# Weight remainders, tanh gates, the adaptive rows' landing place and the opening's small loads in a three-layer kernel

## The chip, the cores and the metric

One NeuronCore of one Trainium2 chip runs the whole program. The metric is the device time of one execution in microseconds; the kernel before took 2408.9 us (median of 3 runs, 2406.74 to 2418.69).

## The reference, cut to what matters

The program runs one layer of a first kind and two of a second on 256 tokens of width 1024. All sums below are of the first layer; the second kind isn't touched, except for where its small vectors are loaded.

```
mod = silu(c) @ w_ada + b_ada            # 6 x 1024 values, from one row c (and c_ctx)
h   = rmsnorm(x) * (1 + scale) + shift   # 256 tokens, and 256 context tokens
q, k, v (attention), q, k, v, o, gates (mLSTM), g_na, g_ml = h @ w_in
a   = neighbourhood attention(q, k, v, context)      # 8 heads
m   = mLSTM(q, k, v, gates), both directions, head norm, * sigmoid(o)   # 4 heads
y   = (sigmoid(g_na) * (a @ w_branch_na) + sigmoid(g_ml) * (m @ w_branch_ml)) @ w_out
x  += gate * rmsnorm(y)
x  += gate * rmsnorm(experts(x))         # 32 experts of 3 x 1024 x 1024, 4 a token
```

## The kernel before, in words

**Engines.** Each engine has its own instruction stream, in program order; semaphores join them. SyncE (SP) issues the weight loads, ScalarE (ACT) issues the small loads at the start and then computes, GpSimd (POOL) issues a few loads, VectorE is DVE, TensorE is PE.

**The ring.** Weights pass through `ring`, 6 slots of 2 MB. `slabs` lists them in order, and slab n goes to slot n % 6; `freed(n)` gives the group of matmuls after which its slot may be overwritten. Four slabs `ada0` to `ada3` hold the first 2048 columns of `w_ada`. Behind the list come the expert slabs, six for each expert (`expert_slab`), j = 0, 1 for `w_gate`, 2, 3 for `w_lin` and 4, 5 for `w_down`.

**Rounded weights and remainders.** A product in float32 is made of three in the faster rounded format: ScalarE writes the rounded weights (`rounded1`, line 740), VectorE the remainder, weight less rounded weight (`rest1`, line 2027), and TensorE multiplies rounded by rounded, rounded by remainder and remainder by rounded. A 1 MB slab has its rounded copy in its own slot; a 2 MB slab (`nav`, `mlv`) has it in the next one (`nav_hi`).

**The rows of w_ada.** `ada0` to `ada3` are multiplied on TensorE (`ada`), copied to SBUF by ScalarE (`ada_copy`, line 716) and turned to columns by TensorE (`ada_turn`, line 1179). Rows 4 to 9 are loaded by GpSimd to `adaX`, two places of 1 MB (line 2701): both halves of a row are issued when the row before has been summed. VectorE sums them (`ada_part`, eight steps, lines 2056 and 2058) and TensorE folds the partitions (`ada_fold`, line 1217); `modulation` adds the bias. Rows 10 and 11 pass through the ring between the gate slabs, and their sums and folds stand in the attention heads (steps i = 1 to 15). The row they are summed in is `cossin`.

**Opening.** SyncE issues the tokens, `ada0`, and after the small vectors `ada1` to `ada3`, `nak0`, `nak1` and `nav`. ScalarE issues 2 + 8 + 1 small loads, and then 16 of the second kind's vectors (`VECS2`) and 10 constants. VectorE waits for the sigmoid of `c` (`sig_c`) ahead of the copies of the turned tokens (lines 1985, 1986). Then come the token norm, the four ada rows, the gains and the rounded tokens (lines 750, 751), and the attention keys, `na_k`, on TensorE (line 1253).

**Projections.** `tokens` (line 1268), `features` (1282) and `lat_pair` (1316) make the other products, with seven groups of small matmuls for the relative bias between them (`rel_group`, line 1230, copied by `rel_copy`) and the folds.

**Heads.** Step i is half qt = i % 2 of head h = i // 2. TensorE: scores of step i + 1 (1370), half of a gate projection (1316), on even steps `head_out` (1379), transposes of the probabilities (1398). VectorE: bias, maximum, scaling, and on odd steps the remainder of a gate slab. ScalarE: exp (803); on odd steps the sigmoid that empties gate h (759) and the rounding of gate h + 2; and the copy of the transposes (820).

**After the heads.** The mLSTM runs head by head with the branch product of attention between (1414, 1426, 1448, 1465); then come its branch product, the output projection (1541) with its norm sums (1501), the router and the experts (from about 440 us; their matmuls are lines 1598 and following). The experts' biases are rounded by ScalarE (892), and their remainder is made by GpSimd (2720). The angles for the second kind stand on VectorE between the remainder of `out3` and the first use of the output projection, which ScalarE's `c_pos` waits for.

## Time and profile before

| | |
|---|---|
| median, lowest, highest of 3 runs | 2408.9, 2406.74, 2418.69 us |
| the profiled execution | 2409.32 us |
| its span, first to last instruction | 2407.5 us |
| mean granted TensorE clock | 0.971 of full |
| TensorE busy | 2201.5 us, 91% |
| VectorE, ScalarE, GpSimd busy | 929.6, 734.7, 28.1 us |
| DMA | 626.98 MB, mean 260 GB/s |
| the first layer up to the experts | 0 to about 440 us |

Times in the rows are microseconds from the start of the span. In the time lines a row with a count merges equal instructions that follow each other, and the brackets give the engine's idle time before it and what ended it. In the busy times the numbers stand in the order PE, PEld (TensorE's weight loads), DVE, ACT, POOL, then the granted clock as a share of full speed, the mean busy share of 16 DMA engines, and GB/s.

### The profile page before, as it was taken

The numbers are of one execution on the slowest core, as the hardware profiler recorded it, in microseconds if no ns is written. First come the engines' busy times: TensorE is split into PE (matmuls) and PEld (weight loads), VectorE is DVE, ScalarE is ACT, GpSimd is POOL, SyncE is SP. The second block draws the span as 40 slices with busy tenths as digits, with TensorE's granted clock in tenths as the row PEclk, the third lists the DMA queues.
The fourth block names the chain that finished last, engine by engine and source line by source line (L and its number), as shares of the span: only waits on it lengthen the run. The fifth ranks groups of instructions, "written<-read, shape, count | busy, mean of one in ns | idle before, by whom it ended". The sixth has DMA issues, their size and how long they took to land.

```text
span 2407.5 us, 33072 instructions
## 1 busy us (share of the span) xinstructions
PE 2201.5 (91%) x13860; PEld 1569.3 (65%) x13860; DVE 929.6 (39%) x1355; ACT 734.7 (31%) x969; POOL 28.1 (1%) x32
## 2 busy tenths in 40 slices
PE   5999888999889888988998899999999799999998
PEld 4887676433333333333333488998999698998997
DVE  4456575311111121111121265366344454474453
ACT  4124552211101111111111245444433444544432
POOL 0000011000000000000000000000000000000000
PEclk8999998999999999999999999999999899999998
DMA  9462156699999999999999934544444454443542
GB/s 359 165 225 90 53 158 212 255 428 427 427 427 428 428 427 428 427 428 428 426 428 428 358 113 159 160 163 153 145 162 167 141 168 148 147 170 137 178 154 92
DMA packets 139388, 626.98 MB, mean 260 GB/s; under 512 B 7703, under 2 KB 33831, under 8 KB 114407
## 3 DMA queue, kind: packets, MB, share of 16 engines
q1 hardware_dynamic: 131808, 609.87, 65.0%
q0 software_dynamic: 5184, 13.90, 2.0%
q8 instruction: 120, 1.97, 0.3%
q10 hardware_dynamic: 2247, 1.01, 0.2%
q14 instruction: 29, 0.24, 0.0%
HBM read 623.69 MB, written 1.05 MB: 259 GB/s over the span
## 4 chain that ended last, share of the span: by engine, by line
PE 65%; DMA 23%; DVE 5%; issue 3%; ACT 3%; SPq 1%; ACTq 0%; DVEq 0%; POOL 0%
DMA ring<-in_w_lin 20%; PE bank L1598 15%; PE bank L1687 12%; PE bank L1922 10%; PE bank L1937 5%; PE bank L1845 3%; DMA ring<-in_w_in 2%; PE bank L1268 2%; PE bank L1316 2%; PE bank L1864 1%; DVE ring_rounded L2027 1%; PE bank L1711 1%; PE bank L1253 1%; PE bank L1696 1%; PE bank L1465 1%
## 5 line engine op out<-in xcount | busy, mean ns | idle before, releaser
L1598 PE MATMUL bank<-ring,arenaA 128*64 128x512 f32 x3072 | 692.9, 601 | 39.3 <-DMA ring<-in_w_lin 28.6
L1598 PEld LDWEIGHTS bank<-ring,arenaA 128*64 128x64 f32 x3072 | 211.0, 138 | 462.1 <-issue 390.3
L2475 DVE TENSOR_TENSOR ring_rounded<-ring,ring_rounded 128x2048 fp32r<-128x2048 f32 (+1 forms) x160 | 338.1, 2152 | 148.1 <-ACT ring_rounded L964 148.1
L964 ACT ACTIVATE ring_rounded<-ring 128x2048 fp32r<-128x2048 f32 (+1 forms) x160 | 280.4, 1799 | 284.7 <-DMA ring<-in_w_in 116.2
L1687 PE MATMUL bank<-arena_rounded,ring_rounded 128*128 128x256 f32 x2496 | 308.9, 284 | 0.0
L1687 PEld LDWEIGHTS bank<-arena_rounded,ring_rounded 128*128 128x128 f32 x2496 | 301.1, 190 | 4.1 <-issue 3.1
L1922 PE MATMUL bank<-arena_rounded,ring_rounded 128*128 128x256 f32 x2112 | 256.0, 282 | 1.2 <-DVE arena_rounded L2665 1.0
L1922 PEld LDWEIGHTS bank<-arena_rounded,ring_rounded 128*128 128x128 f32 x2112 | 252.8, 190 | 4.6 <-ACT arena_rounded L1106 3.0
L2421 DVE TENSOR_SCALAR arenaA<-bank 128x512 f32<-128x512 f32 x32 | 22.1, 692 | 502.4 <-PE bank L1598 502.4
L945 ACT ACTIVATE arenaA<-bank 128x512 f32<-128x512 f32 x32 | 19.1, 597 | 328.8 <-PE bank L1643 328.8
L1937 PE MATMUL bank<-arena_rounded,ring_rounded 128*128 128x256 f32 x912 | 110.0, 283 | 2.3 <-DVE arenaA L2677 2.3
L1937 PEld LDWEIGHTS bank<-arena_rounded,ring_rounded 128*128 128x128 f32 x912 | 109.5, 192 | 2.7 <-issue 2.7
L979 ACT ACTIVATE arenaA<-bank 128x512 f32<-128x512 f32 (+1 forms) x88 | 51.2, 586 | 188.8 <-PE bank L1687 86.9
L949 ACT ACTIVATE arenaA<-bank 64x512 f32<-64x512 f32 x64 | 37.9, 592 | 213.6 <-PE bank L1598 213.2
L943 ACT ACTIVATE arenaA<-arenaA 128x512 f32<-128x512 f32 x32 | 20.2, 630 | 266.3 <-DVE arenaA L2421 266.3
L2433 DVE TENSOR_SCALAR arenaA<-bank 128x512 f32<-128x512 f32 x32 | 22.1, 692 | 201.9 <-PE bank L1598 201.9
L1316 PEld LDWEIGHTS bank<-arena_rounded,ring_rounded 128*128 128x128 f32 x624 | 77.1, 193 | 12.5 <-issue 7.6
L2027 DVE TENSOR_TENSOR ring_rounded<-ring,ring_rounded 128x2048 fp32r<-128x2048 f32 x28 | 70.0, 2513 | 35.6 <-ACT ring_rounded L740 35.5
L1316 PE MATMUL bank<-arena_rounded,ring_rounded 128*128 128x256 f32 x624 | 81.0, 288 | 0.0
L2677 DVE TENSOR_TENSOR arenaA<-bank,arenaA 128x512 f32<-128x512 f32 x22 | 15.2, 691 | 145.5 <-PE bank L1922 145.3
L1611 PE MATMUL bank<-arenaA 128*128 128x256 f32 x256 | 63.5, 392 | 7.8 <-ACT arenaA L949 5.5
L1845 PE MATMUL bank<-arena_rounded,ring_rounded 128*128 128x256 f32 x576 | 70.5, 284 | 0.0
(385 smaller groups left out, 2210.6 us busy)
## 6 DMA issues: line engine op xcount, KB each, us to landing
ring<-in_w_gate SPq DMA_DIRECT2D x64, 2048.0 KB, 23.3
ring<-in_w_lin SPq DMA_DIRECT2D x64, 2048.0 KB, 25.6
ring<-in_w_down SPq DMA_DIRECT2D x64, 2048.0 KB, 21.8
ring<-in_w_in SPq DMA_DIRECT2D x34, 2048.0 KB, 12.0
ring<-in_w_ffn_gate SPq DMA_DIRECT2D x10, 2048.0 KB, 8.1
ring<-in_w_ffn_up SPq DMA_DIRECT2D x10, 2048.0 KB, 7.8
ring<-in_w_ffn_down SPq DMA_DIRECT2D x12, 1536.0 KB, 6.4
ring<-in_w_in SPq DMA_DIRECT2D x16, 1024.0 KB, 8.0
```

Source lines behind the costliest of these rows:

```text
L964: act.activation(place2(name + "_hi", ringR)[:, a:b, :], place2(name)[:, a:b, :], ACT.Copy).then_inc(w_hi, 1)
L979: act.activation(dst, src(b) if src else b, func, scale=scale).then_inc(c_act, 1)
L1268: last = pe.matmul(b[:, :], h(c), w[:, c, :], start=(part == 0 and c == 0), stop=(part == 2 and c == DC - 1), skip_group_check=True)
L1316: last = pe.matmul(b[:, j * T:(j + 1) * T], w[:, c, cols], h(c), start=(part == 0 and c == 0 and j == 0), stop=(part == 2 and c == kc - 1) ...
L1598: last = pe.matmul(bank[b][k * SLOTS:(k + 1) * SLOTS, :], lhsT(c), slot(j)[:, c % 4, k * 512:(k + 1) * 512], start=False, stop=(c == DC - ...
L1611: last = pe.matmul(bank[6 + g % 2][:, k * T:(k + 1) * T], yN[:, c // 4, (c % 4) * P:(c % 4 + 1) * P], selWT, start=True, stop=True)
L1687: last = pe.matmul(b[:, j * T:(j + 1) * T], w[:, c, m * P:(m + 1) * P], h[:, c, :], start=(part == 0 and c == 0 and j == 0), stop=(part == ...
L1845: last = pe.matmul(b[:, j * T:(j + 1) * T], wHL[w][:, c, m * P:(m + 1) * P], y[:, c, :], start=(part == 0 and c == 0 and j == 0), stop=(pa ...
L1922: last = pe.matmul(b[:, j * T:(j + 1) * T], w[:, c, m * P:(m + 1) * P], h[:, c, :], start=(part == 0 and c == 0 and j == 0), stop=(part == ...
L1937: last = pe.matmul(bank[m // 2][:, (m % 2) * T:(m % 2 + 1) * T], w[:, k, m * P:(m + 1) * P], h[:, c0 + k, :], start=(part == 0 and c0 + k ...
L2027: dve.tensor_tensor(lo[:, c, :], w[:, c, :], hi[:, c, :], ALU.subtract).then_inc(w_lo, 1)
L2475: dve.tensor_tensor(place2(name, ringR)[:, a:b, :], w[:, a:b, :], hi[:, a:b, :], ALU.subtract).then_inc(w_lo, 1)
```

## The change

- Opening: `VECS2` and the constants are issued by GpSimd; `mlgRaw` (64 bytes a row) goes behind the first row of `w_ada` there. The token copies of the first four chunks stand ahead of the silu. `VECS2` is turned later, in another bank, and eight matmuls of the identity follow the last `ada_turn`.
- `nak` is one slab of 2 MB with its rounded copy in slot 5.
- Rows 4 to 11 of `w_ada` all pass through `adaX`. Each half has its own semaphore and is loaded as soon as the half before it in that place has been summed. Eight folds stand in the projections, none in the heads; the list ends with two empty slots, and expert 0's slabs are issued in the order 4, 5, 0, 1, 2, 3.
- Heads: a gate is tanh(g / 2), and the products take it plus one; the factor 0.5 moves into `gpost` and the norm's scale. Slabs are rounded on even steps, one step ahead of their remainders; `bna0` and `bna1` are done inside the heads, and the slabs after them move one place ahead.
- The bias remainder is made by VectorE after the remainder of `out3`; ScalarE rounds the biases later.

The diff, cut to changed lines; the places are named:

```diff
# declarations
-adaRow = [Pna[:, 1, :] if i < 4 else wide(AT_MLO, 2, 512, arenaA)[:, i % 2, :] if i < 10 else cossin[:, :]
-          for i in range(12)]
+adaRow = [Pna[:, 1, :] if i < 4 else wide(AT_MLO, 2, 512, arenaA)[:, i % 2, :] for i in range(12)]
...
-ada_in = sem("ada_in")
+ada_in = [sem(f"ada_in{k}") for k in range(2)]
...
-slabs += [(f"nak{i}", half(C_NAK + 256 * i)) for i in range(2)]
-slabs += [("nav", w_in[:, :, C_NAV:C_MLK]), ("nav_hi", None),
+slabs += [("nak", w_in[:, :, C_NAK:C_NAV]), ("nak_hi", None), ("nav", w_in[:, :, C_NAV:C_MLK]), ("nav_hi", None),
...
-for k in range(8):
-    slabs += [(f"gate{k}", half(gate_at[k]))]
-    if k in (0, 2):
-        slabs += [(f"ada{10 + k // 2}", ada_src(10 + k // 2))]
+slabs += [(f"gate{k}", half(gate_at[k])) for k in range(8)]
...
+slabs += [(None, None)] * (-len(slabs) % RING)
...
+PIECES1 = {n: 2 if n in ("nak", "nav", "mlv") else 1 for n in SPLIT1}
# order of the PSUM groups
+ORDER1 = [f"na_k{m}" for m in range(4)] + ["na_v0", "na_v1", "ada4", "na_v2", "ada5", "na_v3", "ml_k0", "ada6", "ml_k1", "ada7",
+                                          "ml_v0", "ml_v1", "ml_v2", "ada8", "ml_v3", "ada9", "ml_g", "ml_q0", "ml_gt", "ada10",
+                                          "na_q0", "ada11", "na_q1", "ml_o0", "ml_o1"]
...
+groups += [("dve" if n.startswith("ada") or n == "ml_gt" else "act", n) for n in ORDER1 + GATES]
# freed, sync: expert 0's slabs
+    while slabs[n][0] is None:
+        n -= RING
...
-    for j in range(RING):
+    for j in (4, 5, 0, 1, 2, 3):
# scalar
-    for L in range(2):
-        for name, (r, k) in VECS2.items():
-            src = A[name][L]
-            src = src if len(src.shape) == 1 else src.rearrange("a b -> (a b)")
-            act.dma_start(vin2[L * NV2 + r:L * NV2 + r + k, :], src.rearrange("(a b) -> a b", b=P)).then_inc(vec2_in, 16)
-    for n in K:
-        if n not in FIRST:
-            act.dma_start(K[n][:, :], A[n]).then_inc(consts_in, 16)
...
-    act.wait_ge(vecs_turned, 2)
-    act.activation(v2T[:, :], bank[6][:, 0:2 * NV2], ACT.Copy).then_inc(v2_copied, 1)
...
+    act.wait_ge(vecs_turned, 2)
+    act.activation(v2T[:, :], bank[4][:, 0:2 * NV2], ACT.Copy).then_inc(v2_copied, 1)
...
-        if PIECES1[name] == 2:
+        if PIECES1[name] == 2 and S1[name + "_hi"] >= RING:
...
-    rounded1("nak0")
+    rounded1("nak", (0,))
...
-    rounded1("nak1")
+    rounded1("nak", (1,))
...
-            empty(GATES[h], dst, ACT.Sigmoid, src=two)
-            if h + 2 < 8:
-                rounded1(f"gate{h + 2}")
-            elif h == 7:
-                rounded1("bna0")
+            empty(GATES[h], dst, ACT.Tanh, scale=0.5, src=two)
+        elif h + 2 < 8:
+            rounded1(f"gate{h + 2}")
+        elif h == 6:
+            rounded1("bna0")
+        else:
+            rounded1("bna1")
...
-        if dr == 1:
-            rounded1(("bna1", "bml0", "bml1", "out0")[h])
+        if dr == 1 and h < 3:
+            rounded1(("bml0", "bml1", "out0")[h])
...
+    rounded1("out1")
...
-    rounded1("out1")
-    act.wait_ge(bias_in, 16 * 6)
-    act.activation(bparts, braw, ACT.Copy).then_inc(bias_hi, 1)
...
+    act.wait_ge(bias_in, 16 * 6)
+    act.activation(bparts, braw, ACT.Copy).then_inc(bias_hi, 1)
...
-        empty_post(bank[g % 4], m, sq2, mixT, gpost, 1.0, lin_act)
+        empty_post(bank[g % 4], m, sq2, mixT, gpost, 0.5, lin_act)
# tensor
-    pe.wait_ge(vec2_in, 16 * 2 * len(VECS2))
-    pe.transpose(bank[6][:, 0:2 * NV2], vin2[0:2 * NV2, :], K["ident"][0:2 * NV2, 0:2 * NV2]).then_inc(vecs_turned, 1)
...
-    pe.wait_ge(v2_copied, 1)
...
+    pe.wait_ge(vec2_in, 16 * 2 * len(VECS2))
+    pe.transpose(bank[4][:, 0:2 * NV2], vin2[0:2 * NV2, :], K["ident"][0:2 * NV2, 0:2 * NV2]).then_inc(vecs_turned, 1)
...
+    pe.wait_ge(v2_copied, 1)
+    for _ in range(8):
+        pe.matmul(bank[4][:, 0:P], K["ident"][:, :], K["ident"][:, :], start=True, stop=True)
...
-        pe.wait_ge(ada_sum, i - 3)
+        pe.wait_ge(ada_sum, 2 * (i - 3))
...
+            if part == 0 and k == 0:
+                wH, wL = highs("nak")
+            if part == 1 and k == 0:
+                lows("nak")
...
-    for t in range(3):
+    for t in range(2):
...
+    tokens("na_v", "nav", 2)
+    ada_fold(5)
...
-    ada_fold(5)
+    ada_fold(6)
...
-    tokens("ml_v", "mlv", 0)
-    tokens("ml_v", "mlv", 1)
-    ada_fold(6)
-    tokens("ml_v", "mlv", 2)
+    ada_fold(7)
+    for t in range(3):
+        tokens("ml_v", "mlv", t)
+    ada_fold(8)
+    ada_fold(9)
-    ada_fold(7)
...
-    ada_fold(8)
+    ada_fold(10)
...
+    ada_fold(11)
...
-    ada_fold(9)
...
-        if i in (8, 14):
-            ada_fold(9 + i // 7)
# vector
-    dve.wait_ge(sig_c, 1)
...
-    dve.tensor_tensor(scol[:, :, 0], vT[:, 0:8], stage[:, 0:8], ALU.mult)
-    dve.tensor_tensor(scol[:, :, 1], vT[:, 8:16], stage[:, 8:16], ALU.mult).then_inc(silu_done, 1)
...
+        if c == 4:
+            dve.wait_ge(sig_c, 1)
+            dve.tensor_tensor(scol[:, :, 0], vT[:, 0:8], stage[:, 0:8], ALU.mult)
+            dve.tensor_tensor(scol[:, :, 1], vT[:, 8:16], stage[:, 8:16], ALU.mult).then_inc(silu_done, 1)
...
-    rest1("nak0")
-    rest1("nak1")
+    rest1("nak")
...
-        if i < 10:
-            dve.wait_ge(ada_in, 32 * (i - 3))
-            w = lambda c: adaX[c // 4][:, c % 4, :]
-        else:
-            dve.wait_ge(*in1(f"ada{i}"))
...
+        w = lambda c: adaX[c // 4][:, c % 4, :]
...
+            if c % 4 == 0:
+                dve.wait_ge(ada_in[c // 4], 16 * (i - 3))
...
-            if c < DC - 1:
+            if c % 4 < 3:
...
+                if c == 3:
+                    dve.wait_ge(ada_sum, 2 * (i - 4) + 1)
...
-    ada_part(5, range(4))
+    ada_part(5, range(4, 8))
+    rest1("mlk")
-    ada_part(5, range(4, 8))
+    modulation(4)
+    ada_part(6, range(8))
-    rest1("mlk")
-    modulation(4)
+    modulation(5)
+    ada_part(7, range(4))
-    rest1("mlv", (0,))
+    ada_part(7, range(4, 8))
-    rest1("mlv", (1,))
-    modulation(5)
-    ada_part(6, range(4))
+    rest1("mlv")
+    modulation(6)
-    ada_part(6, range(4, 8))
+    ada_part(8, range(8))
+    modulation(7)
-    ada_part(7, range(8))
+    ada_part(9, range(8))
-    modulation(6)
...
...
-    ada_part(9, range(4, 8))
...
-        if i in (9, 15):
-            modulation(10 + i // 15)
-        if 1 <= i <= 4:
-            ada_part(10, range(2 * i - 2, 2 * i))
-        if 9 <= i <= 12:
-            ada_part(11, range(2 * i - 18, 2 * i - 16))
-        if qt and h + 2 < 8:
-            rest1(f"gate{h + 2}")
+        if qt:
...
-    rest1("bna0")
...
-        dve.tensor_tensor(merged[:, 2 * h:2 * h + 2, :], two(bank1(f"b_na{h}")[:, :]), gNA[:, 2 * h:2 * h + 2, :], ALU.mult)\
-            .then_inc(lin_dve, 1)
+        dve.scalar_tensor_tensor(out=merged[:, 2 * h:2 * h + 2, :], in0=gNA[:, 2 * h:2 * h + 2, :], scalar=1.0,
+                                 in1=two(bank1(f"b_na{h}")[:, :]), op0=ALU.add, op1=ALU.mult).then_inc(lin_dve, 1)
...
-        rest1(("bna1", "bml0", "bml1", "out0")[h])
+        if h < 3:
+            rest1(("bml0", "bml1", "out0")[h])
...
-        link(dve.tensor_tensor(gm, bank[g % 4][:, :].rearrange("p (a b) -> p a b", a=2), gm, ALU.mult))
+        link(dve.scalar_tensor_tensor(out=gm, in0=gm, scalar=1.0, in1=two(bank[g % 4][:, :]), op0=ALU.add, op1=ALU.mult))
...
+    dve.wait_ge(bias_hi, 1)
+    for k in range(2):
+        r = slice(64 * k + 32, 64 * k + 64)
+        dve.tensor_tensor(bparts[r, :, :], braw[r, :, :], bparts[r, :, :].bitcast(F32), ALU.subtract).then_inc(bias_lo, 1)
...
-    dve.tensor_tensor(gpost[:, :], mod[:, 16:24], vcol("g_mix_post"), ALU.mult)
+    dve.scalar_tensor_tensor(out=gpost[:, :], in0=mod[:, 16:24], scalar=0.5, in1=vcol("g_mix_post"), op0=ALU.mult, op1=ALU.mult)
# gpsimd
-    pool.dma_start(mlgRaw, w_in[:, :, C_MLG:C_NAQ]).then_inc(bg_in, 16)
-    for i in range(4, 10):
-        pool.wait_ge(*((lin_done, G1["ada3"] + 1) if i == 4 else (ada_sum, i - 4)))
+    for L in range(2):
+        for name, (r, k) in VECS2.items():
+            src = A[name][L]
+            src = src if len(src.shape) == 1 else src.rearrange("a b -> (a b)")
+            pool.dma_start(vin2[L * NV2 + r:L * NV2 + r + k, :], src.rearrange("(a b) -> a b", b=P)).then_inc(vec2_in, 16)
+    for n in K:
+        if n not in FIRST:
+            pool.dma_start(K[n][:, :], A[n]).then_inc(consts_in, 16)
+    pool.wait_ge(lin_done, G1["ada3"] + 1)
+    for i in range(4, 12):
-            pool.dma_start(adaX[k], ada_src(i)[:, 4 * k:4 * k + 4, :]).then_inc(ada_in, 16)
+            if i > 4:
+                pool.wait_ge(ada_sum, 2 * (i - 5) + k + 1)
+            pool.dma_start(adaX[k], ada_src(i)[:, 4 * k:4 * k + 4, :]).then_inc(ada_in[k], 16)
+        if i == 4:
+            pool.dma_start(mlgRaw, w_in[:, :, C_MLG:C_NAQ]).then_inc(bg_in, 16)
...
-    pool.wait_ge(bias_hi, 1)
-    for k in range(2):
-        r = slice(64 * k + 32, 64 * k + 64)
-        pool.tensor_tensor(bparts[r, :, :], braw[r, :, :], bparts[r, :, :].bitcast(F32), ALU.subtract).then_inc(bias_lo, 1)
```


## Rows read from the trace of the kernel before

**Rows 1.** The page, part 4: chain that ended last, by engine.

```profile
PE 65%; DMA 23%; DVE 5%; issue 3%; ACT 3%; SPq 1%; ACTq 0%; DVEq 0%; POOL 0%
```

**Rows 2.** By stage: stretch, length, busy us (instructions), granted clock, DMA share, GB/s.

```profile
72.86:201.30 128.44, 126.35 (x733) 107.29 (x731) 60.52 (x79) 34.10 (x35) 7.43 (x10) 0.93 0.62 212
201.30:306.00 104.70, 93.26 (x553) 69.68 (x552) 57.67 (x117) 55.43 (x79) 0.00 (x0) 0.92 0.18 57
```

**Rows 3.** Chain in order of time, opening: start us, us, what.

```profile
23.67 19.27 DMA ring<-in_w_in
42.96 1.37 ACT ring_rounded L740
...
49.09 23.77 PE bank L1253 x96
```

**Rows 4.** Time line, opening: start, us, engine, line, op, tiles, count [idle before].

```profile
1.95 0.90 POOL L2697 DMA_DIRECT2D arenaA<-in_w_in  x1
...
33.82 0.21 ACT L730 ACTIVATE colA<-colA 128x4 f32<-128x4 f32 x1
...
36.17 1.16 PE L1205 MATMUL bank<-k_ident,colA 128*128 128x128 f32 x8 [0.51 <-DVE colA L2007]
...
44.78 0.58 ACT L716 ACTIVATE arenaA<-bank 128x512 f32<-128x512 f32 x1
...
45.41 1.87 PE L1179 MATMUL bank<-k_pick,arenaA 128*128 128x2 f32 x8 [1.13 <-ACT arenaA L716]
```

**Rows 5.** Busy time in a stretch of the opening.

```profile
48.00:50.00 2.00, 0.91 (x2) 0.84 (x3) 2.00 (x2) 2.00 (x5) 1.08 (x2) 0.50 0.99 418
```

**Rows 6.** Time line, projections, TensorE and VectorE.

```profile
67.06 5.48 DVE L2058 SCALAR_TENSOR_TENSOR arenaA<-arenaA,scol 128x512 f32<-128x512 f32 x7
...
67.72 5.15 PE L1253 MATMUL bank<-arena_rounded,ring_rounded 128*128 128x512 f32 x22
...
88.84 7.39 PE L1268 MATMUL bank<-ring_rounded,arena_rounded 128*128 128x512 f32 x24
...
180.93 1.21 PE L1217 MATMUL bank<-ones,arenaA 128*128 128x1 f32 x8 [2.09 <-DVE arenaA L2058]
```

**Rows 7.** One line, GpSimd's ada halves: ns min/median/max, and us to landing.

```profile
L2701 POOL DMA_DIRECT2D arenaA<-in_w_ada x12: 748/751/770, 47.6 to 165.7; - x12
...
DMA to landing us min/median/max: 5.4/7.7/15.1
```

**Rows 8.** Time line, heads, ScalarE.

```profile
260.35 1.91 ACT L740 ACTIVATE ring_rounded<-ring 128x2048 fp32r<-128x2048 f32 x1 [9.99 <-DMA ring<-in_w_in]
```

**Rows 9.** Waits of TensorE, heads: us in total, times, longest.

```profile
PE bank L1379 <- ACT arenaA L820: 10.3, 2, 7.8
```

**Rows 10.** Time line, ScalarE: gates, softmax and table loads.

```profile
171.62 0.26 ACT L782 ACTIVATE arenaA<-arenaA 128x64 f32<-128x64 f32 x1
...
177.89 0.23 ACT L785 ACTIVATE arenaA<-arenaA 128x32 f32<-128x32 f32 x1 [4.07 <-DVE arenaA L2111]
...
214.07 1.28 ACT L759 ACT_TABLE_LOAD   x1 [2.89 <-PE bank L1316]
```

**Rows 11.** Time line, end of the heads.

```profile
300.20 1.94 PE L1379 MATMUL bank<-arenaA 128*64 128x256 f32 x8
...
308.54 3.33 PE L1379 MATMUL bank<-arenaA 128*64 128x256 f32 x8 [2.54 <-ACT arenaA L820]
...
312.37 2.29 DVE L2027 TENSOR_TENSOR ring_rounded<-ring,ring_rounded 128x2048 fp32r<-128x2048 f32 x1
...
320.44 1.16 PE L1426 MATMUL bank<-k_ident,arenaA 128*128 128x128 f32 x8 [0.79 <-ACT arenaA L852]
```

**Rows 12.** Time line, bias remainder and output projection.

```profile
375.32 9.03 POOL L2720 TENSOR_TENSOR arena_rounded<-arenaA,arena_rounded 32x1536 fp32r<-32x1536 f32 x2
375.62 10.87 DVE L2027 TENSOR_TENSOR ring_rounded<-ring,ring_rounded 128x2048 fp32r<-128x2048 f32 x2 [1.12 <-ACT ring_rounded L740]
...
391.72 1.07 PE L1501 MATMUL bank<-arenaA,ones 128*32 128x256 f32 x4 [7.68 <-ACT arenaA L879]
```

39 lines of the change are left out of this document (14 added, 25 removed).

## The prediction, written before the result was known

> **What bounds the kernel now.** I read the page first (the chain that ended last), then busy times by stage, then the chain in order of time and the time lines of the stages that the diff touches. The chain is mostly TensorE (PE), with DMA second [rows 1]; most of that DMA share lies in the expert layer, which no part of the diff makes shorter or longer: expert 0's slabs arrive long before their use, and the later ones are paced by the ring. So the question is by how much the work before about 440 us ends earlier or later; all behind it moves with it. Four stages matter. The opening (0 to 72.86 us) hangs on the transfer of `nak0` and `nak1`: one DMA piece of 19.27 us ends at 42.96 [rows 3]. The projections (72.86 to 201.3) are TensorE almost without a gap, 126.35 of 128.44 us. The attention heads (201.3 to 306) have 104.70 - 93.26 = 11.44 us without TensorE work [rows 2]. After them come short stretches in which TensorE waits for ScalarE or VectorE.
>
> **The change part by part.**
>
> *Opening, small loads.* ScalarE no longer issues 26 small DMAs, so its first ACTIVATE comes earlier; the token copies no longer stand behind the sigmoid. Neither moves the end of the opening: everything waits for `nak`, whose bytes stand in the same queue order. What helps `nak` is that 1024 rows of 64 bytes (`mlgRaw`, issued at 1.95 [rows 4]) no longer run ahead of it, and that it comes in rows of 2 KB instead of 1 KB. Neither has a row of its own. Below: no gain (the stream is as full as before), above: 3.5 us, a sixth of the 19.27 us piece [rows 3]. I take 1.1 us, near the lower end, because the bytes stay the same: landing at 41.9.
>
> *Opening, `nak` as one slab.* Before, `nak0` was rounded while `nak1` was on its way; after it landed only one rounding (1.82) stood before the copy of `ada3` at 44.78 [rows 3, 4]. Now nothing can be rounded until all has landed, and two roundings and the copy of `ada2` stand there: 1.82 + 0.60 + 1.82 = 4.24 instead of 1.82, so 2.4 us later. With the landing, the copy starts at 41.9 + 4.24 = 46.1, 1.3 us later than 44.78. Its followers keep their distances: the turn ended at 45.41 + 1.87 = 47.28 and `na_k` began at 49.09 [rows 3, 4].
>
> *Eight idle matmuls.* They stand on TensorE between the turn of `ada3` (now ending at 48.6) and `na_k`. Four like them take 1.16 us at the full clock [rows 4], so eight take 2.3 us, and 4.6 us at the half clock, which was granted here (0.50 from 48 to 50, [rows 5]). The cover is the 1.8 us between turn and tokens. I take them to end at 51.8, half of them slow, 1.4 us after the tokens are ready (50.4). They give back the slow start of `na_k`: 96 matmuls took 23.77 us [rows 3] and at the later pace (22 in 5.15 us [rows 6], some 0.237 each with the gaps) would take 22.75, 1.0 us less. Opening: +1.3 + 1.4 - 1.0 = +1.7 us; bounds -1.5 and +4.5.
>
> *Halved landing place, eight rows by GpSimd.* Two more `ada_fold` now stand in the projections, 8 matmuls each, 0.9 us: +1.8 us; they leave the heads, where the same 1.8 us goes. VectorE gets two more sums, 6.3 us each (a first step of 0.48 and seven, 5.48 us [rows 6]), into 68 us of idle time (128.44 - 60.52 busy [rows 2]). Each half waits for its own 1 MB, which takes 5.4 to 15.1 us to land, 7.7 in the median [rows 7]. A row needs 3.1 (half a sum) + 0.75 (issue) + 7.7 = 11.6 us, eight take 93 us, and from the first sum at 66.6 to the last fold at about 175 there are 108. The tail is tight. `ada10` takes VectorE's place of `ada8`, whose sum ended just before the last issue pair (165.7 [rows 7]), and the two folds shift it to 166.8; `ada11`'s halves are issued at 164.4 and 167.5, land at about 170 and 174, and its sum ends near 177.4. The last fold was due at 180.93 - 2.09 = 178.8 [rows 6]; one projection (5.8) earlier and two folds later that is 174.8. So the 2.09 us stall of before doesn't go, it becomes about 2.6: +0.5. If all landed in 5.4 it would be 0.8, at 9 us it would be 5. Behind the waiting sum stand the remainders of `mlo0`/`mlo1` and the rope, all due later.
>
> *TensorE's clock in the projections.* A stretch of small matmuls (rel group, with or without a fold) can drop the granted clock: 24 equal matmuls took 7.39 us at 88.84, against 22 in 5.15 [rows 6], and there are four such groups before. With six folds among the groups instead of three I add one drop: +1.5 (bounds -3 and +4.5). Projections in sum: 1.8 + 0.5 + 1.5 = +3.8.
>
> *Heads.* The two slabs `ada10`/`ada11` leave the ring. Before, `gate5` could be loaded only after `ada10`'s fold; ScalarE idled 9.99 us and TensorE 7.8 us [rows 8, 9]. Now `gate5` sits in slot 5, free at 197. Remainders are made a step later and roundings on even steps, where ScalarE has about 5 us to spare of a step pair of 11.2; a table load of 1.28 us before and after each sigmoid goes. The trace shows exp after tanh without a load: tanh at 171.62, exp at 177.89 with none between, against the load at 214.07 before a sigmoid [rows 10]. All that frees is the remaining idle time, since TensorE's own work, 11.2 us a pair, is the floor. Sum: 11.44 idle, 1.7 for the half clock after the long gap, 1.6 for the two folds, less about 0.5 of new small gaps: -14.3.
>
> *End of the heads.* The rounding of `bna0` (1.8 us) leaves the path between the last gate and the last copy, so `head_out` starts at 306.75 instead of 308.54, and with a gap of 0.8 instead of 2.54 us it should keep its clock, 1.94 instead of 3.33 us [rows 11]; the table load and `bna0`'s remainder (2.29) before the first weights go too, so the 0.79 us wait at 320.44 [rows 11] goes. -1.8 - 1.4 - 0.8 = -4.0. What is late next is TensorE's own queue. Before the norm of the mLSTM heads the remainder of `out0` goes; the square-root table load hides all but 0.3: -0.3.
>
> *Bias remainder on VectorE.* The two remainders of `out2` and `out3` took 10.87 us beside GpSimd's 9.03 us [rows 12], against 2.29 each alone [rows 11]. Now 4.5 us, and then the bias remainder, 2 x 1536 elements at 2.29/2048 us = 3.4 us. The work up to `gpost`'s first use ends 10.87 - 4.5 - 3.4 = 2.9 us earlier, and TensorE's wait of 7.68 us [rows 12] shortens by that: -2.9. Below nothing, above 4.
>
> The adds of one, the halved scale and expert 0's slab order: the same instruction counts and times, and some 30 us between landing and use. 0.
>
> **Sum.** 1.7 + 3.8 - 14.3 - 4.0 - 0.3 - 2.9 = -16.0 us. The profiled execution took 2409.3 us (2407.5 of span and 1.8 around it), 0.4 above the median of 2408.9. 2409.3 - 16.0 = 2393.3; against the median 2392.9. I say 2393.
>
> **A rule weighed.** GpSimd issued all twelve ada halves in 0.75 us each, from 47.6 on, whatever VectorE did [rows 7]. The Trainium skill ("SBUF — State Buffer", "SBUF: two separate sides") says that a DMA issued by GpSimd has its descriptors written by that engine, which is locked out while VectorE runs an instruction in a two-port mode, and gives about 0.62 us alone and 3.1 us beside a copy. That speaks against moving 26 small loads there; 16 of them at 3.1 us would put the second layer's vectors at about 58 us instead of 20, an estimate from that page; they are needed by about 40, so the sum would be +18 - 16 = +2.
>
> **Rivals.**
> A. *The opening and the tail of the projections eat more.* Landing unchanged, the idle matmuls all slow (+4), a 5 us stall at the last fold, one more clock drop (+7.5 for the projections): 4 + 7.5 - 21.5 = -10, 2399. For: three of these are bounds, and none is excluded. Against: they must coincide. 0.17.
> B. *The opening gains.* Without the 64-byte rows the stream gains 3 us and no clock drop is added: -0.2 + 1 - 21.5 = -20.7, 2388.5; with the last stall gone 2386. For: the stream moved less in its first 10 us than later. 0.12.
> C. *The landing place sets the pace (slower).* With 8 rows through one place, a landing of 15.1 us [rows 7] makes a row 19 us and seven of them 133 us instead of the 108 there are: +25 on the last fold, less the 16 won: 2418. It decides from a mean landing of about 11.5 us, when the rows just reach the last fold. Against: the 15.1 was in the full stream of the opening; later ones took about half. 0.04.
> D. *GpSimd's issues are slow beside VectorE (slower).* ScalarE waits for the second layer's vectors ahead of the square root (at 33.82 before [rows 4]; with the slack ahead of the tokens it may come at 40). The last of 16 issues must come by 32: 1.88 us each. Rows give 0.75 to 0.9 [rows 4, 7], so vectors at about 20 us. Only GpSimd's tensor work beside VectorE was longer, 4.5 us each [rows 12]; at that price they'd come 40 us late and the time would be 2433. 0.03.
> E. *The tanh doesn't share a table or the slabs stall elsewhere*: gates keep their loads, but the 7.8 us gap still goes: 2397 to 2400. 0.04.
>
> **How the numbers follow.** Forecast 0.60. The range 2384 to 2402 takes in B, A and E and leaves out C and D and 0.10 of misjudged ends. A measurement of this kernel tells 0.5%, 12 us, from no change, so faster means under 2397: the forecast's 0.60 nearly whole (0.57), B 0.12 and a part of A and E (0.06): 0.75. Same: 0.18. Slower: C and D, 0.07.
>
> **What would show it.** Right: no DMA wait of ScalarE between 250 and 260; no table loads between the first exp and the mLSTM; VectorE's two remainders at 2.29 each near 375; the first `na_k` matmul at 50 to 52; a stall of 1 to 4 us at the last fold. Wrong: `na_k` starting before 48 or after 54; a VectorE wait of over 10 us for a half in the projections; more than six slow groups there; heads longer than 92 us; GpSimd's small issues over 1.5 us each.

## The result, and the profile after

The changed kernel took 2392.36 us (median of 6 runs, 2387.57 to 2399.11), beside 2408.24 us for the kernel before in the same session (6 runs, 2402.7 to 2418.69): a ratio of 0.9931, 95% interval 0.9909 to 0.9954. The forecast was 2393 in 2384 to 2402. The profiled execution took 2394.06 us, its span 2391.8, at a mean granted clock of 0.972; so the two profiled executions stand 15.3 us apart, their spans 15.7.

Chain that ended last, by engine, after (before: [rows 1]):

```profile
PE 68%; DMA 23%; DVE 3%; issue 3%; ACT 2%; SPq 0%; ACTq 0%; DVEq 0%
```

What left the chain is mostly VectorE and ScalarE (5% and 3% before). DMA kept its share: most of it lies in the expert layer, where the diff changes only the order of expert 0's slabs.

The opening after, first the chain in order of time, then the time line (columns as in [rows 3, 4]):

```profile
20.85 21.24 DMA ring<-in_w_in
...
46.84 1.87 PE bank L1163 x8
48.71 3.62 PE bank L1198 x16
52.33 22.04 PE bank L1241 x96
```

```profile
46.20 0.59 ACT L700 ACTIVATE arenaA<-bank 128x512 f32<-128x512 f32 x1
...
48.57 3.76 PE L1198 MATMUL bank<-k_ident 128*128 128x128 f32 x16
...
49.29 0.60 ACT L734 ACTIVATE arena_rounded<-arenaA,mod,gains 128x256 fp32r<-128x256 f32 x1 [2.50 <-DVE gains L2006]
```

`nak` landed at 42.09 (42.94 before), the copy of `ada3` came at 46.20, and the idle matmuls (L1198) filled 3.76 us at the half clock where 1.8 us were free. `na_k` ended at 74.38 instead of 72.86.

Busy time by stage after, the projections and the heads (columns as in [rows 2]):

```profile
74.38:206.28 131.90, 131.09 (x749) 111.92 (x748) 72.16 (x97) 34.22 (x35) 9.66 (x13) 0.91 0.65 220
206.28:296.35 90.07, 89.33 (x537) 66.64 (x537) 50.82 (x100) 39.62 (x67) 0.00 (x0) 0.96 0.25 83
```

The projections have next to no gap and still take 131.9 us instead of 128.4; the heads are TensorE throughout, 89.3 of 90.1 us, where 11.4 us were idle up to 306.00 [rows 2] and 2.5 more stood ahead of the last `head_out` [rows 11].

Time line of TensorE, projections after: groups of 24 equal matmuls, the small ones between them, and the last fold (before: [rows 6]):

```profile
82.23 7.41 PE L1256 MATMUL bank<-ring_rounded,arena_rounded 128*128 128x512 f32 x24
89.57 2.43 PE L1218 MATMUL bank<-arenaA,ring 63*128 63x48 f32 x20
91.93 1.05 PE L1205 MATMUL bank<-ones,arenaA 128*128 128x1 f32 x8
92.84 7.38 PE L1256 MATMUL bank<-ring_rounded,arena_rounded 128*128 128x512 f32 x24
...
180.36 1.05 PE L1205 MATMUL bank<-ones,arenaA 128*128 128x1 f32 x8 [0.81 <-DVE arenaA L2043]
```

Such a group takes 5.72 to 5.83 us at the full clock; six took about 7.4 (four before). Each slow one stands behind a rel group (L1218), with or without a fold (L1205). The last fold waited 0.81 us instead of 2.09.

End of the heads and the bias remainder (before: [rows 11, 12]):

```profile
296.35 1.94 PE L1369 MATMUL bank<-arenaA 128*64 128x256 f32 x8 [0.74 <-ACT arenaA L806]
...
307.00 3.29 PE L1436 MATMUL bank<-arenaA 128*128 128x129 f32 x28
...
360.08 4.50 DVE L2016 TENSOR_TENSOR ring_rounded<-ring,ring_rounded 128x2048 fp32r<-128x2048 f32 x2 [1.11 <-ACT ring_rounded L724]
364.61 3.53 DVE L2272 TENSOR_TENSOR arena_rounded<-arenaA,arena_rounded 32x1536 fp32r<-32x1536 f32 x2
...
373.50 1.07 PE L1489 MATMUL bank<-arenaA,ones 128*32 128x256 f32 x4 [4.98 <-ACT arenaA L867]
```

The last `head_out` is at the full clock behind a gap of 0.74 us. VectorE's two remainders take 4.50 us instead of 10.87, the bias remainder 3.53 beside them, and TensorE waits 4.98 instead of 7.68.

The step-by-step balance, from the starts of the same instructions in both time lines (us; the last row is the length of all that follows the experts' first matmul):

| stretch | before | after | change | forecast |
|---|---|---|---|---|
| to the end of `na_k` | 72.86 | 74.38 | +1.5 | +1.7 |
| to the first scores | 128.45 | 131.83 | +3.4 | +3.8 |
| to the last `head_out` | 107.23 | 90.14 | -17.1 | -16.1 |
| to the first mLSTM output | 12.89 | 10.65 | -2.2 | -2.2 |
| to `b_ml` | 36.25 | 35.97 | -0.3 | -0.3 |
| to the first out group | 13.82 | 12.99 | -0.8 | 0 |
| to the first norm sum | 20.22 | 17.54 | -2.7 | -2.9 |
| to the experts | 48.42 | 48.76 | +0.3 | 0 |
| experts to the end | 1967.4 | 1969.5 | +2.2 | 0 |

So the diff took 17.9 us out ahead of the experts. The rest is unchanged code; in the fourteen traces of this case it took 1965.6 to 1971.9 us, so its 2.2 us are scatter. The start of the experts leaves that scatter out and is used beside the medians below. It has a scatter of its own, for each kernel has one trace: with the same code in the stage, the projections took 128.6 to 134.0 us, the heads 90.1 to 91.3, and the stretch to `b_ml` 36.0 or 37.6 (five traces), so its -0.3 us are not shown by these two traces alone.

### The profile page after: what moved, and what is told of

Same layout as the page of the kernel before. It is cut to its first block, busy times and chain, and to the rows that moved or that the text cites. A ratio compares the mean times of both kernels' runs of the same rounds, so it can differ in the third digit from the quotient of the medians.

```text
span 2391.8 us, 33084 instructions
## 1 busy us (share of the span) xinstructions
PE 2209.9 (92%) x13876; PEld 1574.2 (66%) x13876; DVE 928.2 (39%) x1357; ACT 713.0 (30%) x953; POOL 35.5 (1%) x60
## 4 chain that ended last, share of the span: by engine, by line
PE 68%; DMA 23%; DVE 3%; issue 3%; ACT 2%; SPq 0%; ACTq 0%; DVEq 0%
DMA ring<-in_w_lin 20%; PE bank L1586 15%; PE bank L1675 12%; PE bank L1910 11%; PE bank L1925 5%; PE bank L1833 3%; PE bank L1306 3%; PE bank L1256 2%; DMA ring<-in_w_in 2%; PE bank L1699 1%; PE bank L1852 1%; PE bank L1684 1%; PE bank L1241 1%; PE bank L1453 1%; PE bank L1360 1%
## 5 line engine op out<-in xcount | busy, mean ns | idle before, releaser
L1675 PEld LDWEIGHTS bank<-arena_rounded,ring_rounded 128*128 128x128 f32 x2496 | 301.5, 190 | 4.1 <-issue 3.1
L1910 PEld LDWEIGHTS bank<-arena_rounded,ring_rounded 128*128 128x128 f32 x2112 | 254.0, 191 | 4.7 <-ACT arena_rounded L1093 4.0
L1925 PEld LDWEIGHTS bank<-arena_rounded,ring_rounded 128*128 128x128 f32 x912 | 109.5, 192 | 2.7 <-issue 2.7
L1306 PEld LDWEIGHTS bank<-arena_rounded,ring_rounded 128*128 128x128 f32 x624 | 76.6, 191 | 12.4 <-issue 6.8
L1833 PEld LDWEIGHTS bank<-arena_rounded,ring_rounded 128*128 128x128 f32 x576 | 69.5, 192 | 0.0
```

The lines of the kernel that those rows point to most:

```text
L1306: last = pe.matmul(b[:, j * T:(j + 1) * T], w[:, c, cols], h(c), start=(part == 0 and c == 0 and j == 0), stop=(part == 2 and c == kc - 1) ...
L1675: last = pe.matmul(b[:, j * T:(j + 1) * T], w[:, c, m * P:(m + 1) * P], h[:, c, :], start=(part == 0 and c == 0 and j == 0), stop=(part == ...
L1833: last = pe.matmul(b[:, j * T:(j + 1) * T], wHL[w][:, c, m * P:(m + 1) * P], y[:, c, :], start=(part == 0 and c == 0 and j == 0), stop=(pa ...
L1910: last = pe.matmul(b[:, j * T:(j + 1) * T], w[:, c, m * P:(m + 1) * P], h[:, c, :], start=(part == 0 and c == 0 and j == 0), stop=(part == ...
L1925: last = pe.matmul(bank[m // 2][:, (m % 2) * T:(m % 2 + 1) * T], w[:, k, m * P:(m + 1) * P], h[:, c0 + k, :], start=(part == 0 and c0 + k ...
```

## The experiments

All start from the changed kernel. Between brackets in the headings: median us of the kernel, and of the kernel before in the same session.

### Only the ring (2402.02; 2410.22)

Sigmoid, the roundings on odd steps and the bias remainder on GpSimd come back; the landing place and the opening stay.

```diff
-empty(GATES[h], dst, ACT.Tanh, scale=0.5, src=two)          # and the products without the plus one
+empty(GATES[h], dst, ACT.Sigmoid, src=two)
+if h + 2 < 8: rounded1(f"gate{h + 2}")                      # again on odd steps
+pool.tensor_tensor(bparts[r, :, :], braw[r, :, :], ...)     # VectorE's is gone
```

> The changed kernel with sigmoid gates again, roundings and remainders of the gate and branch slabs at their old steps, and the bias remainder on GpSimd: of the change only the landing place for all ada rows (two slabs fewer in the ring) and the new opening stay. Theory (the ring slabs were what held the heads): the stage from the first scores to the start of head_out(7), 107.2 us before and 90.1 in the changed kernel, is 92 to 95 here, with no DMA wait of ScalarE in it; behind it the old end of the heads (+2.2) and the bias wait of 7.7 us come back (+2.7), so the run takes 2399 to 2403 us. Rival (sigmoid's table loads and the crowded odd steps held the heads, the slabs only coincided): the stage stays at 100 us or more and the run takes 2406 or more.

9 runs, ratio to before 0.9966 (0.9955 to 0.9976). First scores to last `head_out`: 204.03 to 300.05, 96.0 us. ScalarE waits for no DMA there. TensorE's waits in the heads and the bias wait, this kernel (us in total, times, longest):

```profile
PE bank L1486 <- ACT arenaA L863: 7.7, 1, 7.7
...
PE bank L1383 <- DVE arenaA L2158: 3.7, 6, 1.6
PE bank L1366 <- ACT arenaA L804: 2.5, 1, 2.5
```

The slabs held the heads: 11.2 of the 17.1 us go with the landing place alone (some 1.6 of them are the two folds that left the stage), and the rival falls. The median lies where the theory put it, the stage 1 us above.

### Sigmoid back (2392.18; 2410.22)

```diff
-empty(GATES[h], dst, ACT.Tanh, scale=0.5, src=two)
+empty(GATES[h], dst, ACT.Sigmoid, src=two)
...   # the products without the plus one, gpost and the norm's scale without the 0.5
```

> The changed kernel with sigmoid in place of the halved tanh and its plus one; all else as changed. Theory: TensorE bounds a pair of head steps (11.07 us) and ScalarE has the table loads beside it, so the inner period stays within 0.2 us of 11.07; only the loads after the last gate and before the first weight exponent are on the path: +1 to +2.5, 2393.5 to 2395. Rival (the loads are what tanh saved): one pair of loads, 2.6 us, reaches the chain of each step pair in part, the period rises to 12 or more and the run takes 2400 or more.

4 runs, ratio 0.9931 (0.9907 to 0.9954). The stage took 206.61 to 297.14, 90.5 us. ScalarE in one pair of steps, this kernel:

```profile
239.06 1.28 ACT L743 ACT_TABLE_LOAD   x1
241.88 0.60 ACT L743 ACTIVATE arenaA<-bank 128x512 f32<-128x512 f32 x1 [1.54 <-PE bank L1306]
242.37 0.59 ACT L806 ACTIVATE arenaA<-bank 128x512 f32<-128x512 f32 x1
242.98 1.28 ACT L787 ACT_TABLE_LOAD   x1
244.28 0.69 ACT L787 ACTIVATE arenaA<-bank,arenaA 128x512 f32<-128x512 f32 x1
244.95 1.91 ACT L724 ACTIVATE ring_rounded<-ring 128x2048 fp32r<-128x2048 f32 x1
```

The loads are there, 1.28 us each, and ScalarE still idles for TensorE in the same steps; the period (one even `head_out` to the next) is 11.06 to 11.09 us, pair by pair the same as with tanh. The 0.4 us more in the stage lie ahead of the first `head_out` and within the scatter of 90.1 to 91.3, so they are not the loads'. What is left is a wait of 0.67 us before the first mLSTM output (0 with tanh): tanh alone is worth some 0.7 us, which the medians can't show, and the expected +1 to +2.5 was too much. The Trainium skill ("ScalarE: Activation LUTs", "What ACT_TABLE_LOAD costs") gives about 1.28 us for a load, as here, and 1.38 us of draining on top. These rows don't show the second part: the load at 242.98 starts 0.02 us after the copy before it ends, and the exponent 0.02 us after the load, 1.32 us in all.

### Roundings back on odd steps (2398.68; 2410.22)

```diff
-elif h + 2 < 8: rounded1(f"gate{h + 2}")     # even steps; elif h == 6: bna0, else bna1
+    if h + 2 < 8: rounded1(f"gate{h + 2}")   # behind the tanh of the odd step; h == 7: bna0
...   # the branch slabs' roundings and remainders one place later again
```

> The changed kernel with the roundings back on the odd head steps, the branch slabs' roundings and remainders one place later as before, tanh kept. Theory: without table loads ScalarE's odd step (exponent, tanh, rounding, copy) still fits beside TensorE, so the inner period grows by less than 0.3 us; the rounding of bna0 stands again between the last gate and the last copy (+1.8) and bna0's remainder before the first weights (+0.5 to 1): +2 to +4, 2394.5 to 2396.5. Rival (even steps are what made the heads tight): period of 11.5 or more, +6 or more.

6 runs, ratio 0.9951 (0.9933 to 0.9969). The stage took 94.7 us, 4.6 more, and its pairs of steps 11.40 to 11.77 us (11.06 to 11.09 in the changed kernel). VectorE and TensorE around an odd step, and TensorE's waits for the softmax in the heads (us in total, times, longest), this kernel:

```profile
239.19 0.60 PE L1383 MATMUL bank<-k_ident,arenaA 128*128 128x128 f32 x4
241.82 2.29 DVE L2013 TENSOR_TENSOR ring_rounded<-ring,ring_rounded 128x2048 fp32r<-128x2048 f32 x1 [3.54 <-ACT ring_rounded L724]
244.03 0.43 DVE L2136 TENSOR_TENSOR bank<-bank,arenaA 128x256 f32<-128x256 f32 x1
...
245.48 0.49 DVE L2158 TENSOR_SCALAR arenaA<-arenaA 128x512 f32<-128x512 f32 x1
```

```profile
PE bank L1383 <- DVE arenaA L2158: 2.4, 6, 0.6
```

VectorE stands 3.54 us in front of the remainder, because ScalarE rounded that slab in the same step; the softmax of the next step (to L2158) queues behind it, and TensorE's transposes wait, 2.4 us in six times. With the rounding a step ahead the remainder finds its input ready. The gap of 2.5 us and the half clock at the last `head_out` (3.05 us) come back too. From the first scores to the experts this kernel took 221.4 us, the changed one 216.1: 5.4 us, of them 4.6 in the heads, more than was expected; in the median it was 6. Period and price are the rival's.

### The bias remainder back on GpSimd (2395.37; 2410.22)

```diff
-dve.tensor_tensor(bparts[r, :, :], braw[r, :, :], bparts[r, :, :].bitcast(F32), ALU.subtract)
+pool.tensor_tensor(bparts[r, :, :], braw[r, :, :], bparts[r, :, :].bitcast(F32), ALU.subtract)
...   # both in a loop over k; ScalarE rounds the biases ahead of the sums again
```

> The changed kernel with the bias remainder on GpSimd again, next to VectorE's remainders of out2 and out3, and its rounding ahead of the sums on ScalarE. Theory: the two engines' tensor operations on SBUF slow each other; VectorE's two remainders take 10 to 11 us instead of 4.5, TensorE's wait ahead of the bias matmuls is 7.7 instead of 5.0: +2.7, 2395. Rival (GpSimd's remainder ran for nothing on the path and VectorE's slowness has another cause): the remainders stay at 4.5 to 5 us, the wait falls to 2 us or less, -3.

4 runs, ratio 0.9936 (0.9913 to 0.9959). This kernel, GpSimd, VectorE and TensorE:

```profile
362.30 9.03 POOL L2715 TENSOR_TENSOR arena_rounded<-arenaA,arena_rounded 32x1536 fp32r<-32x1536 f32 x2
362.59 10.89 DVE L2016 TENSOR_TENSOR ring_rounded<-ring,ring_rounded 128x2048 fp32r<-128x2048 f32 x2 [1.11 <-ACT ring_rounded L724]
...
378.71 1.07 PE L1489 MATMUL bank<-arenaA,ones 128*32 128x256 f32 x4 [7.69 <-ACT arenaA L867]
```

As the theory said, to a tenth: GpSimd's work beside VectorE's makes 4.50 us into 10.89, and costs 2.7 us.

### The opening: nak in two slabs (2392.86; 2411.56), no idle matmuls (2394.49), the loads as before (2396.21)

```diff
# nak in two slabs, each rounded when it lands
-slabs += [("nak", w_in[:, :, C_NAK:C_NAV]), ("nak_hi", None),
+slabs += [(f"nak{i}", half(C_NAK + 256 * i)) for i in range(2)]
# no idle matmuls
-for _ in range(8):
-    pe.matmul(bank[4][:, 0:P], K["ident"][:, :], K["ident"][:, :], start=True, stop=True)
# the loads as before
-pool.dma_start(...)   # VECS2, constants
+act.dma_start(...)    # VECS2, constants; mlgRaw as GpSimd's first large load
```

> The changed kernel with nak in two slabs of 1 MB again, each rounded when it lands; the idle matmuls, the order of the loads and the rest as changed. Theory (with one slab the rounding of the first half waits for all 2 MB): the second slab lands at 42 to 43 and one rounding instead of two stands behind it, the copy of ada3 comes 1.5 to 2.4 us earlier than 46.20, the projections start at 50 to 50.5 instead of 52.3: -1.5 to -2, 2390.5. Rival (the last tokens and the idle matmuls set the start, not the copy): start at 52 or later, no change.

> The changed kernel without the eight idle matmuls ahead of na_k, the wait for the second layer's vectors kept. They ran from 48.57 to 52.33 at the low clock, and the first rounded tokens were there by about 50.3. Theory (they cover no clock, they only stand in the way): na_k starts at 50.3 to 50.6 and runs 0.5 to 1.4 us longer, its end comes 0.5 to 1.5 us earlier. Rival (they bring the clock up for what follows): na_k starts 1.9 us earlier but ends no earlier or up to 1 us later, and a further slow group shows behind it.

> The changed kernel with the 26 small loads issued by ScalarE again, ahead of its first activation, and mlgRaw as GpSimd's first large load; nak in one slab, the token copies ahead of the sigmoid, the idle matmuls as changed. Theory (the 64-byte rows of mlgRaw run ahead of the slabs and ScalarE's issues delay its squares): nak lands at 42.5 to 43.5 instead of 42.11, ada(0) starts 1 us or more later than 19.18, the projections start 0.5 to 1.2 us later. Rival (the stream of slabs is full either way and only its bytes count): landing and start within 0.3 us of the changed kernel's, no change of the time.

The ratios are 0.9924 (0.9907 to 0.9940), 0.9933 (0.9917 to 0.9950) and 0.9940 (0.9923 to 0.9956), too close to each other and to the changed kernel's to be told apart. The traces show more. Two slabs: one rounding of 1.91 us at 39.73, the second at 42.73, and `na_k` starts at 50.32 instead of 51.98; the group behind it starts at 73.14 instead of 74.21, and in no trace with one slab before 74.08. By the experts' start (422.36) nothing of it is left in this trace; behind the heads it lost 1.6 us in the stretch to `b_ml`, as one of the five traces with 37.6 there. The start is where the theory put it; the 1.5 to 2 us don't show in the median.

No idle matmuls: `na_k` starts at 50.90 behind a wait of 1.82 us and takes 24.22 us. Busy time from 50 to 52 and from 52 to 56 us, first the kernel without the idle matmuls (all engines), then the changed kernel (TensorE alone); and `na_k` in the changed kernel, without the idle matmuls, and in the kernel with the bias remainder on GpSimd, whose opening is the changed one's:

```profile
50.00:52.00 2.00, 1.10 (x3) 0.94 (x4) 2.00 (x2) 2.00 (x5) 1.77 (x3) 0.50 1.08 438
52.00:56.00 4.00, 4.00 (x13) 3.11 (x12) 4.00 (x7) 4.00 (x9) 0.00 (x0) 0.59 0.97 408
```

```profile
50.00:52.00 2.00, 2.00 (x12) 0.50 0.99 406
52.00:56.00 4.00, 4.00 (x19) 0.94 0.99 414
```

```profile
51.98 22.39 PE L1241 MATMUL bank<-arena_rounded,ring_rounded 128*128 128x512 f32 x96
```

```profile
50.90 24.22 PE L1239 MATMUL bank<-arena_rounded,ring_rounded 128*128 128x512 f32 x96 [1.82 <-ACT arena_rounded L735]
```

```profile
52.42 23.21 PE L1241 MATMUL bank<-arena_rounded,ring_rounded 128*128 128x512 f32 x96
```

The idle matmuls run at 1.2 GHz to the end, and what follows them comes to 2.4 GHz sooner: in the nine traces with this opening the clock from 52 to 56 us was 0.66 to 0.94, without them 0.59, and `na_k` took 22.4 to 23.2 us instead of 24.2. But it also started later, at 52.0 to 52.5. The group behind it started at 74.2 to 75.5 in the nine and at 74.96 without, in the midst of them. So my theory fell, for they do cover clock, and what they give back (1.0 to 1.9 us) is about what they cost (1.1 to 1.5): a net gain is not shown, nor a loss. The rival's further slow group didn't come either (five, six in the changed kernel).

The loads as before: `nak` lands at 42.14, as with the change (42.11), though `ada(0)` starts at 22.11 instead of 19.18; `na_k` starts at 52.08. The order of the small loads moves nothing that counts, the rival's case, and the 1.1 us that the forecast gave to the 64-byte rows isn't theirs: `nak` lands 0.85 us earlier than before with these rows in front or behind. In two slabs it landed at 42.71, so 0.6 of it goes with the one transfer in rows twice as wide; the rest stays open. The median of this kernel, 3.9 us above the changed one's, shows in its trace only behind the opening: 2.0 us by the first scores, with a clock of 0.82 from 74 to 140 us (0.84 with the change) and a wait of 1.5 us at the last fold.

### The rel groups in pieces: ten (2402.78; 2411.56), two (2386.98; 2411.36), three (2388.95)

```diff
# after the large matmul number `after` of a projection group
+REL_CUT = {11: 5, 23: 5}                 # two pieces; three: {7: 3, 15: 3, 23: 4}
-    rel_group(REL_AFTER[name])
+    rel_group(REL_AFTER[name], after)     # ten pieces: one matmul behind every second large one
```

> The changed kernel with the ten small matmuls of each rel group no longer in one piece behind a projection group, but one behind every second large matmul of the same group; the folds stay in their places. In the changed kernel six groups of 24 matmuls took about 7.4 us instead of 5.8 (four before). Theory (TensorE's granted clock falls behind an unbroken piece of small matmuls, 2.43 us of rel group and 0.9 of fold): with the pieces gone at most one or two slow groups stay, the projections take 6 to 9 us less and the run 2384 to 2387. Rival (the small matmuls cost clock wherever they stand, or each switch between the two shapes costs a stall): as many matmuls run at the low clock as before, the projections take as long or up to 5 us longer, 2392 to 2397.

> The changed kernel with each rel group cut in two: five of its ten small matmuls after the twelfth large one, five at the old place. With one small matmul behind every second large one the granted clock stayed at 1.00 over the projections, and they still took 139.4 us instead of 131.9: 64 pieces instead of 7 cost some 18 us, 0.3 us for each further piece, and the clock gave 9 to 11 back. Theory (both hold, the clock falls only behind long pieces): seven further pieces cost 2.2 us, the slow groups go from six to two or fewer (-6 to -9): the projections take 125 to 128 us, the run 2385 to 2389. Rival (five in a row, and the folds beside them, are long enough): as many slow groups as before and 2.2 us more, 134 us and 2394 to 2396.

> The changed kernel with each rel group cut in three (3, 3 and 4 small matmuls, after the eighth, sixteenth and last large one). Theory: 13 further pieces at 0.3 us cost 4 us, no slow group is left (-9 to -11): the projections take 125 to 127 us, the run 2385 to 2388. Rival (the cost of a piece is larger when the piece is short, or the folds alone keep the drops): 132 us or more, no gain.

Ratios: ten pieces 0.9966 (0.9952 to 0.9980), two 0.9899 (0.9882 to 0.9915), three 0.9911 (0.9891 to 0.9931). The projections, end of `na_k` to first scores, with ten pieces, and then with two (changed kernel above: 131.90 us at 0.91):

```profile
75.67:215.05 139.38, 138.69 (x750) 103.01 (x748) 72.10 (x97) 34.34 (x35) 8.99 (x12) 1.00 0.62 205
```

```profile
75.46:198.61 123.15, 122.39 (x748) 103.74 (x748) 72.16 (x97) 34.21 (x35) 8.99 (x12) 1.00 0.70 233
```

Both are at the full clock throughout, no group of 24 is slow; but each switch from large to small matmuls and back costs about 0.3 us (64 pieces against 13: 16.2 us for 51), and ten of them in a group cost more than the clock gives. With ten pieces each theory was half right, the first on the clock, the rival on the switches, and the run (2402.78) lies above both ranges. With two, the projections are 8.7 us shorter than in the changed kernel and 5.3 shorter than before the change, 2 us under the expected range; with three (20 pieces) they take 125.3, by the same price. The clock drops were the price of the form of these groups, not of the projections: 123 and 125 us lie well outside the 128.6 to 134.0 of the nine traces with the groups in one piece. The Trainium skill ("TensorE: Matmul & The Clock Gate", "HAM oscillation — how this bites in real kernels") tells of such drops where the engine idles between tiles; here they come with TensorE busy 131.1 of 131.9 us, which that section doesn't cover.

### The angles first (2388.11; 2411.36)

```diff
# VectorE: gpost, gpre and the angles (to c_pos) now stand ahead of
+rest1("out2")
+rest1("out3")
+dve.tensor_tensor(bparts[r, :, :], braw[r, :, :], ...)
```

> The changed kernel with VectorE's fifteen small operations on the gains and the position angles ahead of the remainders of out2 and out3 and of the bias. In the changed kernel they ran from 368.17 to 372.8, behind those remainders, and ScalarE's first emptying of an out group waited for them, and TensorE 4.98 us for ScalarE. Theory (that queue order on VectorE is what is late after the bias remainder left GpSimd): the wait of TensorE falls under 0.5 us, the remainders of out2 still come before their group: -4.5 to -5, 2387 to 2388. Rival (TensorE then waits for the remainder of out2 instead, or the angles wait for their positions' load): the time comes back there, within 1.5 us of the changed kernel.

4 runs, ratio 0.9902 (0.9885 to 0.9919). TensorE, this kernel:

```profile
358.39 10.22 PE L1529 MATMUL bank<-arena_rounded,ring_rounded 128*128 128x256 f32 x84 [0.75 <-ACT arena_rounded L880]
368.54 0.62 PE L1489 MATMUL bank<-arenaA,ones 128*32 128x256 f32 x4
369.10 5.95 PE L1529 MATMUL bank<-arena_rounded,ring_rounded 128*128 128x256 f32 x48
```

The wait of 4.98 us is gone and doesn't return; the next group has the full clock (5.95 us instead of 6.94). The experts start at 415.81 instead of 422.26; the median fell by 4.3 us.

### All three together (2378.78; 2408.91)

`nak` in two slabs, two pieces, the angles first.

> The changed kernel with the three edits that the traces so far show as gains: nak in two slabs (start of the projections 50.32 instead of 51.98), rel groups cut in two (run 5.4 us below the changed kernel's median), VectorE's angles ahead of the remainders (4.3 us). Theory (they lie in separate stages and each keeps its cover): they add up, 1.3 + 5.4 + 4.3 = 11, 2381 to 2382. Rival (with the projections 7 us shorter the landing place of the eight rows sets the last fold, so that the earlier start comes back as a longer stall there): that stall grows to 3 us or more and the run takes 2383 to 2386.

4 runs, ratio 0.9877 (0.9858 to 0.9895). The edits add up, to more than the 11 us expected: the experts start at 407.26, 15.0 us before the changed kernel's, and the last fold's wait doesn't grow:

```profile
171.60 1.05 PE L1206 MATMUL bank<-ones,arenaA 128*128 128x1 f32 x8 [0.76 <-DVE arenaA L2055]
```

It beats both kernels, the one before by 30 us.

## Why the prediction was right, point by point

**Small loads and landing.** Landing 42.11 for 41.9: right by number, not by reason. The row width and `mlgRaw`'s place were given 1.1 us, and with the old order the landing was the same. Rival D falls, its condition never came near: GpSimd's 26 small issues took 0.50 to 0.56 us each, where it needed 1.88. The last four ran while VectorE copied tokens; time line after:

```profile
13.53 0.41 DVE L1975 COPY arenaA<-bank 128x256 f32<-128x256 f32 x1
13.63 0.54 POOL L2692 DMA_DIRECT2D k_invfreq<-in_invfreq  x1
13.97 0.42 DVE L1974 COPY xT<-bank 128x256 f32<-128x256 f32 x1
14.16 0.54 POOL L2692 DMA_DIRECT2D cossin<-in_cos  x1
```

The rule of the Trainium skill that was weighed ("SBUF — State Buffer", "SBUF: two separate sides"), some 3.1 us for such an issue beside a copy, doesn't show in these four, whose copies read PSUM. No small issue stood beside a copy that reads SBUF, so the rule itself isn't tested here.

**One slab and idle matmuls.** The copy at 46.20 for 46.1, the start of the projections at 52.33 on the chain for 51.8, the sum +1.5 for +1.7. The slab costs its time (two slabs end `na_k` 1 us earlier). "Half of them slow" was wrong, all of the idle matmuls were; but all slow they took 3.76 us, not the 4.6 that the prediction gave for that case, so they ended at 52.33, near the forecast 51.8. They cost about what they give back.

**Landing place.** Two folds more, +1.8, as forecast. The last stall fell from 2.09 to 0.81 us instead of growing to 2.6, and so one of the signs of being right, a stall of 1 to 4 us, didn't come: halves landed in 5.9 us in the median over all sixteen, not 7.7. The prediction's own reckoning gives 0.8 for 5.4. Rival C falls with that. One line, GpSimd's halves after (columns as in [rows 7]):

```profile
L2698 POOL DMA_DIRECT2D arenaA<-in_w_ada x16: 751/751/762, 49.0 to 171.4; - x16
...
DMA to landing us min/median/max: 5.4/5.9/15.2
```

**The clock in the projections.** One more drop, +1.5, was forecast; two came, +3.0. That term was mis-sized, and the stall's 1.3 us in the other direction hid it: +3.4 for +3.8. It is also not a constant: in the nine traces with the same projections' code four to six groups were slow, some of them for 8.2 to 8.7 us, and the stage took 128.6 to 134.0 us. The ring kernel had four and 128.6 us, no more than before. That the forecast came within 0.4 us here is luck.

**Rivals A and B.** Of A one part came true, the idle matmuls all slow, and not its price. Of B the earlier landing came by 0.85 us only, and two clock drops were added, where it wanted none.

**Heads.** -17.1 for -16.1. The mechanism was the slabs', as forecast ([rows 8, 9]): 11.2 us. Where I was vague, in the 1.7 and the "new small gaps", the runs divide the rest: 1.3 us tanh on odd steps (94.7 instead of 96.0, all of it in the first pair of steps, 11.50 instead of 12.77), 4.6 the roundings a step ahead, of which 1.8 is `bna0` as forecast and most of the other the odd step's chain through VectorE (2.4 us of waits), which I didn't see. The order matters: with the roundings ahead, tanh gains nothing in the heads. "A table load before and after each sigmoid goes" was right as a fact (18 loads from 200 to 345 us with sigmoid, 2 without) and was worth nearly nothing, for they lie beside TensorE. Rival E's first half falls in this sense: had the loads stayed, the time would have been the same to 0.7 us.

**After the heads.** -2.2 and -0.3 came as forecast. The -0.8 ahead of the first out group was not in the sum: `b_ml` and what stands behind it ran at 0.88 of the full clock instead of 0.82. The waits ahead of it were 4.29 and 0.45 us instead of 4.56 and 0.49; whether that is the reason is not shown. The bias remainder, -2.7 for -2.9, is shown by its own run.

**The whole.** Ahead of the experts -17.9 for -16.0; the rest added 2.2 by scatter. That the forecast lies only 0.6 us from the median is partly luck. Two slips of the working move nothing: a sixth of 19.27 us is 3.2, not 3.5, and the terms of the heads add up to 14.2, not 14.3.

## What to carry to other kernels

Cost a stage by the wait that ends last in it: here two slabs that TensorE had to release itself were worth 11 us, and 16 table loads on an engine with idle time 0.7. When an engine makes an input and another uses it in the same step, the step after it pays; make it one step ahead. Small matmuls put between large ones have two prices, a granted clock that falls behind a long piece and a switch of about 0.3 us for each piece, so try two or three cuts before leaving them in one.

## What the runs showed that I had not expected

- A rel group in one piece of 2.43 us, in two of 1.31 or in ten: the granted clock of the projections was 0.91, 1.00 and 1.00, and the stage took 131.9, 123.2 and 139.4 us.
- Eight matmuls of the identity at the half clock, 3.76 us, left the next 4 us at 0.66 to 0.94 of the full clock instead of 0.59, and what followed `na_k` started no earlier for it.
- The stretch from the experts to the end, the same code in all traces, took 1965.6 to 1971.9 us. What differs by less than 3 us in a median of this kernel has to be read in the trace, and there against the same stage in the other traces: one pair of traces alone would have called the idle matmuls a gain of 0.7 us.
- The three further edits gave 15.0 us ahead of the experts, nearly as much as the whole change.
